# The last fixed expert round is run behind the loop, its rows added by a one-hot product and the others' pairs summed on GpSimd

## What is computed

```python
def hier_moe(x, norm_g, router_g, router_g_b, router_e, router_e_b, exp_w1, exp_w3, exp_w2):
    xt = rms_norm(x, norm_g).reshape(n * t, D_MODEL)
    ...
    top_v, top_i = lax.top_k(e_sel, TOP_K_IN_GROUP)          # 2 of the 8 experts of one group
    top_w = jax.nn.softmax(top_v, axis=-1) * p_g[:, None]
    ...
    for g in range(N_GROUPS):                                # 4 groups of 8 experts
        h1 = jnp.einsum('td,edf->tef', xt, exp_w1[g])        # D_MODEL 1024, EXPERT_FF 256
        h3 = jnp.einsum('td,edf->tef', xt, exp_w3[g])
        act = jax.nn.silu(h1) * h3 * comb[:, g, :, None]
        out = out + jnp.einsum('tef,efd->td', act, exp_w2[g])
    return x + out.reshape(n, t, D_MODEL)
```

## Time and profile before

| | us |
|---|---|
| median of 3 runs | 661.59 |
| lowest to highest | 661.56 to 664.11 |
| the profiled execution | 662.47 |
| its span | 660.7 |
| TensorE's granted clock over the span, share of full speed | 0.967 |

### The profile page before, as it was taken

How to read it: one execution, slowest core, us unless ns; L and a number is a source line. 1 busy time by engine, 2 the same in 40 slices (tenths; PEclk the granted TensorE clock), 3 DMA queues, 4 the chain that set the end, 5 groups by cost and what they waited for, 6 DMA issues and landing times.

```text
span 660.7 us, 11996 instructions
## 1 busy us (share of the span) xinstructions
PE 598.9 (91%) x4918; PEld 476.6 (72%) x4918; DVE 324.8 (49%) x668; ACT 186.4 (28%) x319; POOL 71.2 (11%) x144
## 2 busy tenths in 40 slices
PE   8999999999999999998999989998999999578930
PEld 8999997677899999984788878555655556236610
DVE  5669799889643464676713165312212221112116
ACT  5523223245834344436003050111011101000103
POOL 1000000000002200000302211211121111102010
PEclk9999999999999999999999998999999999979985
DMA  8762210326554223659769688899999999999927
GB/s 321 295 282 92 101 65 2 131 87 215 167 159 170 101 92 129 255 217 377 299 239 395 260 310 330 353 416 417 418 421 419 420 420 419 420 420 420 400 97 314
DMA packets 35523, 179.46 MB, mean 272 GB/s; under 512 B 8967, under 2 KB 10407, under 8 KB 16645
## 3 DMA queue, kind: packets, MB, share of 16 engines
q1 hardware_dynamic: 26317, 163.19, 62.7%
q0 software_dynamic: 5600, 12.76, 5.0%
q10 hardware_dynamic: 3552, 2.75, 1.3%
HBM read 172.85 MB, written 15.61 MB: 285 GB/s over the span
## 4 chain that ended last, share of the span: by engine, by line
PE 72%; DMA 11%; DVE 6%; issue 5%; SPq 4%; ACT 1%; POOL 0%; DVEq 0%; POOLq 0%; ACTq 0%
PE ps L2228 13%; PE ps L1779 13%; PE ps L1781 12%; PE ps L1780 12%; PE ps L2257 7%; DMA w<-exp_w 4%; PE ps L1893 4%; PE ps L1775 3%; SPq L660 3%; DMA q_rows<-q_s 2%; DMA raw<-weights 2%; DMA qb<-q_rows 2%; PE ps L1850 1%; DMA yr<-y_rows 1%; PE ps L2059 1%
## 5 line engine op out<-in xcount | busy, mean ns | idle before, releaser
L1779 PE MATMUL ps<-xH,w_h 128*128 128x260 f32 x480 | 138.3, 288 | 0.3 <-DVE xL L1417 0.3
L1781 PE MATMUL ps<-xL,w_h 128*128 128x260 f32 x480 | 135.6, 283 | 0.0
L1780 PE MATMUL ps<-xH,w_l 128*128 128x260 f32 x480 | 135.4, 282 | 0.0
L2228 PE MATMUL ps<-w,xeT 128*64 128x256 f32 (+2 forms) x1024 | 116.9, 390 | 9.5 <-DMA w<-exp_w 7.3
L2228 PEld LDWEIGHTS ps<-w,xeT 128*64 128x64 f32 (+2 forms) x1024 | 80.8, 139 | 49.1 <-issue 21.9
L1779 PEld LDWEIGHTS ps<-xH,w_h 128*128 128x128 f32 x480 | 90.4, 188 | 5.1 <-issue 4.3
L1780 PEld LDWEIGHTS ps<-xH,w_l 128*128 128x128 f32 x480 | 90.3, 188 | 0.3 <-issue 0.2
L1781 PEld LDWEIGHTS ps<-xL,w_h 128*128 128x128 f32 x480 | 90.4, 188 | 0.0
L1098 DVE TENSOR_TENSOR w_l<-raw,w_h 128x2048 fp32r<-128x2048 f32 x27 | 61.8, 2288 | 28.2 <-ACT w_h L779 28.1
L2257 PE MATMUL ps<-w,aT 128*64 128x512 f32 (+2 forms) x256 | 60.3, 627 | 15.8 <-DVE aT L1688 12.7
L779 ACT ACTIVATE w_h<-raw 128x2048 fp32r<-128x2048 f32 x27 | 51.6, 1911 | 21.9 <-PE ps L1781 18.9
(11 more groups left out here) (375 smaller groups left out, 862.3 us busy)
## 6 DMA issues: line engine op xcount, KB each, us to landing
w<-exp_w SPq DMA_DIRECT2D x96, 1024.0 KB, 22.6
raw<-weights SPq DMA_DIRECT2D x27, 1024.0 KB, 5.3
raw<-caches SPq DMA_DIRECT2D x16, 1024.0 KB, 6.1
qb<-q_rows POOLq DMA_DIRECT2D x4, 1024.0 KB, 7.5
yr<-y_rows SPq DMA_DIRECT2D x4, 1024.0 KB, 8.4
xT<-x_turned SPq DMA_DIRECT2D x4, 520.0 KB, 7.5
raw<-x_prompt SPq DMA_DIRECT2D x4, 512.0 KB, 12.4
x_rows<-x ACTq DMA_DIRECT2D x4, 512.0 KB
```

The lines of the kernel that those rows point to most:

```text
L1779: pe.matmul(out, h1, h2, start=start, stop=False)
L1780: pe.matmul(out, l1, h2, start=False, stop=False)
L1781: return pe.matmul(out, h1, l2, start=False, stop=stop)
L2228: last = pe.matmul((mm[0][half, j, 0:FF], ta[1][half, 0:FF])[h], xeT[j][:, k, half], w13[s][:, h, k, :], start=k == 0, stop=k == KT_D - 1)
```

## The change

The fixed rounds get the kinds `PPPPSPPPSQSQSP`. The last of them, round 13 (`LATE`, a P round with places 26 and 27), is no longer run with the others. Its rows are gathered and turned before the loop, into a third buffer `xeT[2]`, but its products run behind the loop. Its weights are loaded last, after those of the loop's four experts. Its result rows are not scattered: at the start zeros are scattered to their places in `y_rows`, and behind the loop they are added to each token by a product with a 0/1 matrix (`hot_late`, which says which row belongs to which token), in `late_rows`. The other rounds' rows are read back as before, and their two rows per token are summed on GpSimd. DVE adds the product's result to that sum (`add_late`). The late round uses `xe[3]`, which rounds 3, 7 and 11 use as well. SP's instructions for reading `y_rows` back do not wait for the late round.

```diff
-for kind in "PPPPSPPPSQSPQS":
+for kind in "PPPPSPPPSQSQSP":
     p = ROUNDS[-1][-1] + 1 if ROUNDS else 0
     ROUNDS.append(tuple(range(p, p + {"S": 1, "P": 2, "Q": 4}[kind])))
 PAIRS = len(ROUNDS)
 FIXED = 28
-assert ROUNDS[-1][-1] + 1 == FIXED and PAIRS % 2 == 0
+assert ROUNDS[-1][-1] + 1 == FIXED
+LATE = PAIRS - 1
+LATE_PLACES = ROUNDS[LATE]
+LOOP_J = (LATE % 2, (LATE + 1) % 2)
...
-FREE_AT = [max(ROUND_OF[FIXED + 2 * r + n - RING] for n in range(2)) + 1 for r in range(2)]
+BEFORE_LOOP = LATE_PLACES[0]
+LOOP_SLOTS = [(BEFORE_LOOP + n) % RING for n in range(4)]
+LATE_SLOTS = [(BEFORE_LOOP + 4 + n) % RING for n in range(2)]
+assert len(LATE_PLACES) == 2
+FREE_AT = [max(ROUND_OF[BEFORE_LOOP + 2 * r + n - RING] for n in range(2)) + 1 for r in range(3)]
...
+        xeT.append(at("xeT2", [P, KT_D, P], F32, zone[4]))
+        token_row = at("token_row", [P, T], F32, zone[4] + 2 * 4096)
+        hot_late = at("hot_late", [P, SEQ], F32, zone[4] + 3 * 4096)
+        hot_s = at("hot_s", [P, NS, NS * NS + 1], F32, zone[4] + 4 * 4096 + 2048)
+        hot_s_rows = hot_s[:].rearrange("p c w -> p (c w)")
...
-        LOOP_ROWS = (PAIRS % ROWS, (PAIRS + 1) % ROWS)
+        LOOP_ROWS = (LATE % ROWS, (LATE + 1) % ROWS)
+        LATE_ROWS = (LATE + 2) % ROWS
+
+        def late_sums(t):
+
...
+            return len(range(i, q, ROWS)) + int(i == LATE_ROWS)
+
+        def gathered(i, q):
...
-            for q, places in enumerate(ROUNDS):
-                coming = [p + RING for p in places if p + RING < FIXED]
+            for q, places in enumerate(ROUNDS[:LATE]):
+                coming = [p + RING for p in places if p + RING < BEFORE_LOOP]
...
+            which = [expert_at(p) for p in LATE_PLACES]
+            for h, free in enumerate((gate_ready, hid_ready)):
+                sp.wait_ge(free, FREE_AT[2])
+                for i, e in zip(LATE_SLOTS, which):
+                    load_half(i, e, h)
+            sp.wait_ge(y_done, FREE_AT[2])
+            for i, e in zip(LATE_SLOTS, which):
+                load_down(i, e)
...
+                if t == 1:
+                    sp.dma_start(fin_g[:], a["final_norm_g"].rearrange("(o d) -> o d", o=1).broadcast_to([P, D])).then_inc(fg_in, 16)
+                    sp.dma_start(fin_gs[0:N_PARTS], a["final_g_parts"]).then_inc(fg_in, 16)
+            for t, (t0, n) in enumerate(TILES[:3]):
+                sp.wait_ge(y_out, t + 1)
+                sp.dma_start(y_prompt[0, t0:t0 + n, :], yo[t][:]).then_inc(y_saved, 16)
+            sp.wait_ge(y_out, 4)
...
+            columns_left(LATE, 2, LATE)
...
+            silu_of(loops_n * 2 + LATE, LOOP_J[0], of_slot[:, 0, LATE:LATE + 1])
...
+            columns_right(LATE, 2, LATE)
...
+            dve.wait_ge(route_made, 6)
+            link(dve.tensor_copy(late_no[:], gids[:, LATE:LATE + 1]))
+            dve.tensor_scalar(hot_late[:], token_row[:, 0:SEQ], late_no[:, 0:1], None, ALU.is_equal)
+            of_sample = token_row[:, SEQ:T].rearrange("p (o t) -> p o t", o=1).broadcast_to([P, NS, NS])
+            own_parts = hot_s[:, :, 0:NS * NS].rearrange("p c (t e) -> p c t e", e=NS)[:, :, :, 0]
+            dve.tensor_scalar(own_parts, of_sample, late_no[:, 0:1], None, ALU.is_equal)
+            late = loops_n * 2 + LATE
+            gate_of(late, LOOP_J[0], of_slot[:, 0, LATE:LATE + 1])
+            act_columns_out(late)
+            rows_out(late, LATE_ROWS, of_slot[:, 1, LATE:LATE + 1])
+
+            def add_late(t):
+
+                dve.wait_ge(y_pair, t + 1)
+                dve.wait_ge(y_total, t + 1)
+                row = x2[:, t, :].rearrange("p (b f) -> p b f", b=2)
+                dve.tensor_tensor(row, late_sums(t)[:], row, ALU.add).then_inc(y_sum, 1)
...
+            for t in range(3):
+                add_late(t + 1)
+                dve.wait_ge(y_sq, t + 1)
+                mean_of(fin_ss[:, t:t + 1], fin_ss[:, t:t + 1])
+                factor_of(fin_ss[:, t:t + 1], t + 1)
+                normed(t, slice(0, D))
...
+            gathered_columns(LATE_ROWS, gathered(LATE_ROWS, LATE) + 1)
             pe.wait_ge(pass_ready, 1)
             loops_n = pe.value_load(more[0:1, 0:1], min_val=1, max_val=MORE_ITEMS // 4)
+            pe.wait_ge(xa_ready, LATE + 1)
+            pe.wait_ge(xv_ready, LATE + 1)
             with pe.Fori(0, loops_n) as it:
...
+            late = loops_n * 2 + LATE
+            slots = [(i, (BEFORE_LOOP + 4 + n) // RING + 1) for n, i in enumerate(LATE_SLOTS)]
+            hidden(late, LOOP_J[0], slots, turned=(LATE + 1, xeT[2]))
+            act_columns(late)
+            down(late, slots)
+
+            def late_rows(t, b):
+
+                return pe.matmul(late_sums(t)[:, b, :], hot_late[:, t * P:(t + 1) * P], xe[LATE_ROWS][:, 512 * b:512 * b + 512],
+                                 start=True, stop=True)
+
+            pe.wait_ge(y_ready, loops_n * 4 + (2 * LATE + 1))
+            late_rows(0, 0)
+            late_rows(1, 0)
+            pe.wait_ge(y_ready, loops_n * 4 + (2 * LATE + 2))
+            late_rows(0, 1).then_inc(y_total, 1)
+            late_rows(1, 1).then_inc(y_total, 1)
+            for t in (2, 3):
+                if t == 3:
+                    pe.wait_ge(y_sum, 1)
+                for b in range(2):
+                    last = late_rows(t, b)
+                last.then_inc(y_total, 1)
             pe.wait_ge(yr_in[4], 16)
-            pe.matmul(ta[1][0:N_PARTS, 0:PART], two_rows[:].rearrange("p t c -> p (t c)"), yr_s[:], start=True,
-                      stop=True).then_inc(y_total, 1)
-            pe.wait_ge(y_sq, 1)
+            pe.matmul(ta[1][0:N_PARTS, 0:PART], two_rows[:].rearrange("p t c -> p (t c)"), yr_s[:], start=True, stop=False)
+            for c in range(NS):
+                last = pe.matmul(ta[1][0:N_PARTS, 0:PART], hot_s_rows[:, c * NS * NS:(c + 1) * NS * NS], xe[LATE_ROWS][:, c * PART:(c + 1) * PART], start=False,
+                                 stop=c == NS - 1)
+            last.then_inc(y_total, 1)
...
+            scatter(LATE_ROWS, ids[:, LATE:LATE + 1])
+            for q in range(LATE):
                 pool.wait_ge(xt_done, q + 1)
-                i = (q + 2) % ROWS
-                if q + 2 >= ROWS:
+                i, column = (q + 2) % ROWS, q + 2 + int(q + 2 >= LATE)
+                if scattered(i, q + 2):
                     pool.wait_ge(y_stored[i], 16 * scattered(i, q + 2))
-                gather(i, gids[:, q + 2:q + 3])
+                gather(i, gids[:, column:column + 1])
+                if q == LATE - 1:
+                    pool.wait_ge(y_stored[LATE_ROWS], 16 * scattered(LATE_ROWS, LATE))
+                    gather(LATE_ROWS, gids[:, LATE:LATE + 1])
                 pool.wait_ge(y_ready, 2 * (q + 1))
                 scatter(q % ROWS, ids[:, q:q + 1])
+            pool.memset(hot_s_rows[:, 0:NS * NS * NS], 0.0).then_inc(route_made, 1)
+            pool.iota(token_row[:], pattern=[[1, T]], base=0, channel_multiplier=0,
+                      allow_small_or_imprecise_dtypes=True).then_inc(route_made, 1)
...
+            for t in range(4):
+                pool.wait_ge(yr_in[t], 16)
+                pool.tensor_tensor(x2[:, t, :], yr[t][:, 0, :], yr[t][:, 1, :], ALU.add).then_inc(y_pair, 1)
```

More of the change, by code:

```diff
@@ L1021, in _, with columns_left @@
             act.activation(w_ex[:, 0, :], w_ex[:, 0, :], ACT.Exp).then_inc(g_exp, 1)
-            def columns_left(q, j, old=True):
+            def columns_left(q, j, read=None):
                 act.wait_ge(xt_done, q + 1)
-                if old:
-                    act.wait_ge(hid_ready, q - 1)
+                if read is not None:
+                    act.wait_ge(hid_ready, read)
                 for k in range(4):
@@ L1651, in _, with columns_right @@
             gk_b = gk[:, 4:8].rearrange("p (k o) -> p k o", o=1).broadcast_to([P, 4, P])
-            def columns_right(q, j, old=True):
+            def columns_right(q, j, read=None):
                 dve.wait_ge(xt_done, q + 1)
-                if old:
-                    dve.wait_ge(hid_ready, q - 1)
+                if read is not None:
+                    dve.wait_ge(hid_ready, read)
                 dve.tensor_tensor(xeT[j][:, 4:8, :], tv[1].rearrange("p (k t) -> p k t", k=4), gk_b, ALU.mult).then_inc(xv_ready, 1)
-            columns_right(0, 0, False)
+            columns_right(0, 0)
             dve.wait_ge(route_by_pe, ROUTE_BY_PE["of_slot"])
@@ new lines, in mean_of, with factor_of, normed @@
+            def mean_of(ss, total):
+                dve.tensor_scalar(ss, total, 1.0 / D, 4.0 * EPS, ALU.mult, ALU.add).then_inc(y_ms, 1)
+            def factor_of(ss, n):
+                dve.wait_ge(y_root, n)
+                link(dve.reciprocal(ss, ss))
+            def normed(t, c):
+                dve.scalar_tensor_tensor(yo[t][:, c], x2[:, t, c], fin_ss[:, t:t + 1], fin_g[:, c],
+                                         ALU.mult, ALU.mult).then_inc(y_out, 1)
+            add_late(0)
+            dve.wait_ge(fg_in, 32)
@@ new lines, in _ @@
```

(36 more changed lines are left out.)

141 lines of the change are left out of this document (56 added, 85 removed).

## The result

The changed kernel takes 667.93 us (median of 10 runs, 665.03 to 669.91), the kernel before in the same rounds 662.29 (10 runs, 660.42 to 664.11). The ratio is 1.0078, with a 95% interval of 1.0058 to 1.0099: **slower by 5.6 us**. The forecast was slower, 672.2, with a range of 665 to 678. The time is in the range. The point is 4.3 us too high, and as a change, +10.6 against +5.6, it is almost twice the measured one: it started from the 661.59 of the first three runs, and the same kernel takes 662.29 in ten.

The account below looks back on a forecast made before the run. Bound by the weight stream at the Q round's weights only, behind it by PE's own work. −10.1 + 12.6 + 2.7 + 8.9 + 2.0 − 5.5 = +10.6 on the profiled 662.47 gave 673.1, 672.2 as median; range 665 to 678.

Parts of the forecast that it names:

- X: End of the Q round's down products; with two places fewer to wait for, predicted 10.1 us earlier, at 584.5.
- stand: PE idle behind the S round until the late rows, gathered into xe[3] after the Q round's scatter, land: +8.9 us.
- tail: From the last expert product to the span's end: 20.1 us instead of 25.6, so −5.5.
- second turn: At the loop's entry PE turns the late rows, waits for the copies, and does it again: +2.7 us.
- clock: PE's granted clock falls in its idle time and slows the products after it: +2.0 us, bounds 0 and 4.
- extra P round: One more P round behind the Q round, S, P, P, P instead of S, P, P: +12.6 us.
- The late gather: Chain into xe[3]: scatter at X + 1.6, landed 8.2 later, gather 0.9 later, landed 10.5 later; X + 21.2 in all.
- rival 2: Clock stays at 1.2 GHz through the loop's first round, 5 us in place of 2.0, late chain slower: 677; chance 0.10.
- E: End of the last expert product, predicted at 651.2 us, with all four GpSimd sums ending after it.
- rival 3: Blocked writes: DVE's normalised writes stand behind GpSimd sums, 2.6 us at most: 673.5 to 674.8; chance 0.10.
- Rival 1: No stand at the loop's entry, late rows landing by X + 12.3: 661.3, chance 0.12, or 657.7, chance 0.06.

Follow-up runs that it names:

- experiment 1: The changed kernel with the late rows in xe[1] and the loop's rows in xe[2] and xe[3]: 659.83 us, ratio 0.9985 to the kernel before.
- experiment 2: The changed kernel with 42 and 10 unused small products on PE before and behind the late rows' turn: 669.58 us, ratio 1.0111.
- experiment 4: The changed kernel with GpSimd's sums ahead of its waits for the two surplus gathers: 667.29 us, ratio 1.0093.
- Experiment 3: The kernel before with the new order of kinds PPPPSPPPSQSQSP alone, no round behind the loop: 667.92 us, ratio 1.0096.
- experiment 5: The changed kernel with 24 and 5 unused small products on PE before and behind the late rows' turn: 665.66 us, ratio 1.0058.
- experiment 7: experiment 1 with the Q round last before the loop (PPPPSPPPSQSSQP) and GpSimd's sums ahead of its surplus-gather waits: 655.82 us, ratio 0.9916.

## Why the prediction was right, and where its sizes were off

The mechanism held: a gain ahead of X, a stand of PE behind the S round, a shorter tail. Its six terms, from the start of the fixed rounds, measured in one execution each:

| term | predicted | measured | from |
|---|---|---|---|
| X | −10.1 | −12.5 | 171.3 − 183.9 |
| stand | +8.9 | +6.2 | (598.08 − 579.55) − (606.87 − 594.58) |
| second turn | +2.7 | +2.5 | 5.13 in experiment 1 (597.36 − 592.23), 2.67 before |
| clock | +2.0 | +3.3 | 6.87 − 5.13 for the turns, 8.68 − 7.13 |
| extra P round | +12.6 | +12.6 | (644.66 − 604.95) − 25.59, less 1.55 |
| tail | −5.5 | −6.2 | 19.3 − 25.6 |
| sum | +10.6 | +5.8 | with the unrounded terms |

(6.87 is 604.95 − 598.08, from the late turn to the first hidden product. The measured terms are stretches of one execution, so they add up to 5.8 by construction.)

The sum came out 4.8 us too high. The stand has 2.7 of it, X 2.4, the tail 0.7 and the second turn 0.2; the clock, put too low by 1.3, took some of it back.

*The Q round.* The order of the weight loads does set it: in six kernels with the change's order and its late loads of places 26 and 27, X is 170.6 to 173.1 from the start, where I had put 183.9 − 10.1 = 173.8. The 2.4 us too few are 0.7 more than the bound that I gave. 1.7 of them is what that bound names: the down products kept the clock (3.64, not 5.34). My central value took the slow ones, though nothing said that the shorter wait would again drop the clock. The count by megabytes was right to 0.7 us. In experiments 1, 2 and 4 `w2` is there before PE wants it; the wait for `w3` and the slow products behind it (5.16 to 6.35 us) set X there. Experiment 3 bears it out from the other side: there place 26 is still in the group of the Q round's last loads, so that place 24's `w2` is the 10th megabyte and not the 8th, and X comes 4.2 us later than in the changed kernel.

*The late gather.* **This is the step with the largest error.** Scatter at X + 1.6 as said, landed 8.0 later (8.2), the gather 0.7 behind it (0.9), landed **8.2** later where I took the median of 10.5. With the smaller differences the stand is 2.7 shorter. This gather goes out alone, while those of the median go out 0.3 us behind a scatter; the one of the same kind in experiment 1 landed after 7.9. Whether that is the reason was not tried. The range of 6.1 to 11.2 held the landing, but the prediction took only 1.2 us off for the whole chain as its lower bound, and gives no working for it. With the shortest landings of the earlier trace rows the chain is 5.0 shorter; the 2.7 measured lies outside the bound and inside those rows.

*The clock.* I took the cost of one group of products after a wait, 2.05. But three groups ran at the lower level: both turns (0.9 each more) and the first part of the hidden products. In experiments 1 and 5 all three run at full speed. The bound of 4 held. That the clock stays low through the loop's first round (rival 2) did not happen: at 608 the stretch shows 0.97.

*The extra round.* 12.6 was right to the tenth. Experiment 3 shows what it does to the trade: the order costs 6.3 us by the ratio and 4.7 from the start in the kernel before, without any late round.

*The tail.* DVE waited 0.77 us for the second sum, not 1.9: the sums start 0.1 behind E, not 0.6, the first two take 4.7 together where I had 5.2, and DVE's first add came 0.2 later. As forecast, all four sums end behind E.

The blocked writes of rival 3 did come, but short. Three instructions take longer than their kind, and each starts while one of the other engine is under way. DVE's first write starts at 651.29, 0.5 before the third sum ends, and takes 1.57 us instead of 1.28. The fourth sum starts at 651.72, 1.1 before that write ends, and takes 3.36 instead of 2.36. The second write starts at 654.53, 0.5 before the fourth sum ends, and takes 1.63. Experiment 5 has a write that meets a sum with 1.2 us left (the sum's row is that of a window that ends before the next one, so that it stands alone):

```profile
646.71 2.35 POOL L2537 TENSOR_TENSOR x<-yr 128x1024 f32<-128x1024 f32 x1 [0.68 <-DMA yr<-y_rows]
```
```profile
647.87 2.28 DVE L1788 SCALAR_TENSOR_TENSOR yo<-x,fin_ss,fin_g 128x1024 f32<-128x1024 f32 x1
```

The sum, which began first, keeps its 2.35 us; the write takes 1.0 longer. In experiment 7 it is the other way round, the write starts first:

```profile
637.61 1.28 DVE L1789 SCALAR_TENSOR_TENSOR yo<-x,fin_ss,fin_g 128x1024 f32<-128x1024 f32 x1
```
```profile
637.97 3.12 POOL L2533 TENSOR_TENSOR x<-yr 128x1024 f32<-128x1024 f32 x1 [2.20 <-DMA yr<-y_rows]
```

This sum is the first of the two in the merged row of 5.43 above; the other takes 2.34. Each time the later one is longer by what was left of the earlier one, less some 0.2 us. DVE's adds, which read one operand from PSUM, are no longer for a sum beside them: 1.23 at 647.54. The rule of the Trainium skill ("SBUF — State Buffer", section "SBUF: two separate sides") says that of a DVE operation with two SBUF inputs and a GpSimd operation that reads SBUF the one that starts first goes through and the other waits; the trace agrees. The rival's price was 2.6 at most. Here the two writes lost 0.3 and 0.35, 0.6 in all, since each met only the end of a sum; in experiment 5 they lost 1.35. The prediction also says that no DVE instruction overlaps a GpSimd sum in the kernel before. Two of the thirteen sums do overlap one (at 246.7 and 364.7); the others take 1.30 to 1.33 us, so its price stands on them.

*Rival 1*, no stand, came to life in experiment 1, and with it the time that it gave: 661.3 or, with X's clock kept, less; measured 659.83. Stand and clock, priced at 10.9 together, were 9.5 in the trace, and undoing them gave 8.9 by the trace and 6.2 by the ratios. The rival was wrong of the changed kernel as it stands, but what it named as decisive, a landing by X + 12.3, is what another choice of buffer gives.
